# Two transformer blocks on one core: attention portions moved among k-steps, window scores of two heads in one portion, gate weights in one operand

## The reference

```python
# first block, per layer
h = rms_norm(x, g_pre);  proj = h @ w_in            # 2048 -> 6 k columns, split into heads
o_a = dense attention, 8 heads of 128, 2 key heads, norm and rope on q and k, * silu(a_g)
o_b = dense attention, 4 heads of 128+64, q and kv from low-rank latents,      * silu(b_g)
o_c = neighbourhood attention, 4 heads of 128, bias per position,             * silu(c_g)
x = x + rms_norm(concat(o_a, o_b, o_c) @ w_out, g_post)
# second block, per layer
h = rms_norm(x, g_pre) * (1 + scale) + shift;  proj = h @ w_in
y_a = sliding-window attention: 16 query heads of 64, 4 key heads, window 128, sinks
y_b = gelu(s_u) * spatial gating of gelu(s_v), chunks of 128
gate_logits = c_g @ gla_w_gate_up + gla_b_gate      # c_g: 16 columns of proj
log_alpha   = log_sigmoid(gate_logits) / 16
y_c = rms_norm(gated_linear_attention(c_q, c_k, c_v, log_alpha))
x = x + gate * rms_norm((concat(y_a, y_b, y_c) * silu(z)) @ w_out, g_post)
```

## Time and profile before

| | us |
| --- | --- |
| median of 3 runs | 3762.35 |
| lowest and highest | 3760.0, 3763.01 |
| the profiled execution's own time | 3766.83 |
| its span in the trace | 3765.1 |
| PE busy in it | 3553.3 (94%) |
| DVE, ACT, POOL busy | 1718.8, 1141.5, 1139.8 |
| mean granted clock of PE | 0.975 |

### The profile page before, as it was taken

The page is one execution under the profiler, slowest core; times in us unless marked ns, Lnnn a source line. Parts: engine busy times, 40 slices in busy tenths (PEclk is TensorE's granted clock), DMA queues, the critical chain, the costliest instruction groups (busy, mean ns, idle before and its releaser), DMA issues.

```text
span 3765.1 us, 52278 instructions
## 1 busy us (share of the span) xinstructions
PE 3553.3 (94%) x17005; PEld 2819.4 (75%) x17005; DVE 1718.8 (46%) x2884; ACT 1141.5 (30%) x1918; POOL 1139.8 (30%) x1242
## 2 busy tenths in 40 slices
PE   6999999999799999999997999999997999999998
PEld 5767777778686677777786778877786878877786
DVE  4533476443444236654425335544535334545533
ACT  3122333322321333332323234322323224322221
POOL 5664776560175477765300000012000000002000
PEclk9999999999899999999998999999998999999999
DMA  7444444453354354434432311322433322321332
GB/s 248 127 118 128 141 138 118 120 180 112 131 175 118 88 160 141 137 112 148 158 99 101 95 57 57 95 59 65 159 101 109 96 61 57 95 65 52 122 135 100
DMA packets 184717, 430.87 MB, mean 114 GB/s; under 512 B 21238, under 2 KB 26257, under 8 KB 178328
## 3 DMA queue, kind: packets, MB, share of 16 engines
q1 hardware_dynamic: 146344, 292.60, 24.7%
q0 software_dynamic: 33472, 109.06, 10.3%
q10 hardware_dynamic: 4656, 26.07, 1.8%
HBM read 406.58 MB, written 24.75 MB: 115 GB/s over the span
## 4 chain that ended last, share of the span: by engine, by line
PE 89%; DVE 5%; issue 3%; ACT 1%; DMA 1%; DVEq 0%; ACTq 0%; SPq 0%; POOL 0%; POOLq 0%
PE bank L699 22%; PE bank L701 21%; PE bank L700 21%; PE bank L772 4%; PE bank L792 3%; PE bank L758 2%; PE bank L878 2%; PE bank L694 2%; PE bank L781 2%; PE bank L696 1%; PE bank L695 1%; PE bank L718 1%; PE bank L899 1%; PE bank L1031 1%; PE bank L950 1%
## 5 line engine op out<-in xcount | busy, mean ns | idle before, releaser
L699 PE MATMUL bank<-wlo,act_hi 128*128 128x512 f32 (+1 forms) x3712 | 1531.8, 413 | 1.5 <-DVE zone L1530 0.9
L701 PE MATMUL bank<-whi,act_lo 128*128 128x512 f32 (+1 forms) x3712 | 1448.0, 390 | 0.0
L700 PE MATMUL bank<-whi,act_hi 128*128 128x512 f32 (+1 forms) x3712 | 1446.6, 390 | 0.0
L1475 DVE TENSOR_TENSOR wlo<-stage,whi 128x1024 fp32r<-128x1024 f32 (+1 forms) x496 | 670.0, 1357 | 730.1 <-ACT whi L1116 718.2
L699 PEld LDWEIGHTS bank<-wlo,act_hi 128*128 128x128 f32 x3712 | 704.1, 190 | 205.8 <-issue 63.2
L700 PEld LDWEIGHTS bank<-whi,act_hi 128*128 128x128 f32 x3712 | 704.7, 190 | 153.4 <-issue 24.7
L701 PEld LDWEIGHTS bank<-whi,act_lo 128*128 128x128 f32 x3712 | 702.5, 189 | 149.1
L1116 ACT ACTIVATE whi<-stage 128x1024 fp32r<-128x1024 f32 (+1 forms) x496 | 514.0, 1044 | 779.7 <-PE bank L701 381.6
L2291 POOL TENSOR_TENSOR macc<-macc,mprod 128x512 f32<-128x512 f32 x360 | 497.5, 1382 | 66.5 <-POOL mprod L2284 66.5
L2284 POOL TENSOR_SCALAR mprod<-wmod,csil 128x512 f32<-128x512 f32 x384 | 310.2, 808 | 296.6 <-PE bank L815 192.8
L2328 POOL DMA_DIRECT2D macc<-in_gla_w_gate_up x2 | 1.1, 542 | 1189.2 <-DVE Y L1948 1189.2
(11 more groups left out here) (255 smaller groups left out, 3244.0 us busy)
## 6 DMA issues: line engine op xcount, KB each, us to landing
stage<-in_w_in SPq DMA_DIRECT2D x352, 512.0 KB, 3.7
wmod<-in_w_mod POOLq DMA_DIRECT2D x384, 256.0 KB, 3.1
stage<-in_w_out SPq DMA_DIRECT2D x128, 512.0 KB, 3.8
out<-Y ACTq DMA_DIRECT2D x20, 1024.0 KB, 5.0
zone<-out SPq DMA_DIRECT2D x4, 4096.0 KB, 14.9
stage<-in_w_in SPq DMA_DIRECT2D x16, 320.0 KB, 3.7
Y<-in_x SPq DMA_DIRECT2D x4, 1024.0 KB, 10.2
rpb_tiles<-rpb_pad POOLq DMA_DIRECT2D x16, 224.0 KB, 4.9
```

The lines of the kernel that those rows point to most:

```text
L699: pe.matmul(out, hi_x, lo_w, start=(k == 0), stop=False)
L700: pe.matmul(out, hi_x, hi_w, start=False, stop=False)
L701: mm = pe.matmul(out, lo_x, hi_w, start=False, stop=(k == KC - 1))
L1475: dve.tensor_tensor(wlo[:, j % RH, :, 0:width], stage[:, j % RS, :, 0:width], whi[:, j % RH, :, 0:width].bitcast(F32), ALU.subtract).then_ ...
```

## The change

Lines of the changed kernel from L671 on are 7 to 10 higher than before.

- First block: the steps of units and jobs move. No scores are issued on steps whose `pv` would fall on k = 4 or 5, so none on k = 0 and 1; `UNIT_PV` goes from 3 to 4. The jobs of branch B come 1 to 3 steps later, AK goes from s = 112 to 117, AQ to a new list, the norms and ropes 1 to 3 steps later.
- Second block, window scores: the scores of the duos d and d + 1 are issued in one portion, on the step of the even d, the two heads by turns. Duos 0 and 1 of a quad are now the two heads of the first token pair. The wait is for the exponential of d (d - 1 counted from the duo ahead), the queries' wait for that of 4g.
- c_g: `cgw_hi` and `cgw_lo` become the two halves of one operand of 32 columns, `JOB_CG` has 32 matmuls, the gate matmul contracts over 32 rows with `gate_w` loaded twice.
- Levels: the steps skip k = 15 and k = 0, and what hangs on them moves along.

```diff
+UNIT_TURN, UNIT_PV, ROW_SUM = 2, 4, 4
+def unit_steps(first, n):
+    free = [s for s in range(first, first + 2 * n) if (s + UNIT_PV) % KC not in (ROW_SUM, ROW_SUM + 1)]
+    return free[:n]
+AQ_JOBS = (124, 131, 136, 141, 148, 153, 158, 165)
-for first, steps in ((U_B, [48, *range(51, 64), 64, 67]), (U_C, [*range(83, 97), 99, 100]),
-                     (U_A, [123, 124, 125, 126, 128, 131, 132, 133, 135, 136, 137, 138, 140, 141, 142, 143,
-                            147, 148, 149, 150, 152, 153, 154, 155, 157, 158, 159, 160, 163, 164, 165, 166])):
+for first, steps in ((U_B, unit_steps(50, 16)), (U_C, unit_steps(83, 16))):
     UNIT_AT.update({s: first + i for i, s in enumerate(steps)})
-UNIT_TURN, UNIT_PV = 2, 3
+for h in range(A_H):
+    UNIT_AT.update({s: U_A + 4 * h + i for i, s in enumerate(unit_steps(AQ_JOBS[h] + 1, 4))})
-for first, steps in ((J_CQ, (20, 21, 22, 23)), (J_QPE, (24, 25, 26, 27)), (J_QN, (28, 29, 30, 31)),
-                     (J_QPT, (33, 33, 34, 34)), (J_CKV, (35, 36, 37)), (J_KN, (38, 39, 40, 41)),
-                     (J_VB, (42, 43, 44, 45)), (J_AK, (112, 113)), (J_AQ, (122, 127, 134, 139, 144, 151, 156, 161))):
+for first, steps in ((J_CQ, (23, 24, 25, 26)), (J_QPE, (27, 28, 29, 30)), (J_QN, (31, 32, 33, 34)),
+                     (J_QPT, (36, 36, 37, 37)), (J_CKV, (38, 39, 40)), (J_KN, (41, 42, 42, 43)),
+                     (J_VB, (43, 44, 44, 45)), (J_AK, (117, 118)), (J_AQ, AQ_JOBS)):
-CQ_AT, QROPE_AT, CKV_AT = 17, 28, 32
+CQ_AT, QROPE_AT, CKV_AT = 17, 31, 35
-A_LOAD_AT, AK_AT, AQ_AT = 105, 106, (114, 130)
+A_LOAD_AT, AK_AT, AQ_AT = 105, 107, (116, 131)
...
-LEVEL_AT = 74
-OUT_AT = {91: 0, 93: 1, 106: 2, 108: 3}
-SQ_AT, SCALE_AT = 110, 113
+LEVEL = [s for s in range(74, 120) if s % KC not in (KC - 1, 0)][:4 * (LEVELS + 1) + 1]
+OUT_AT = {LEVEL[17]: 0, LEVEL[19]: 1, LEVEL[28] + 3: 2, LEVEL[28] + 5: 3}
+SQ_AT, SCALE_AT = LEVEL[28] + 7, LEVEL[28] + 10
...
-        score_done = count("score_done", UNITS, DUOS)
+        score_done = count("score_done", UNITS, DUOS // 2)
...
-            return 8 * (g // 4) + g % 4 + 4 * (d % 4 // 2)
+            return 8 * (g // 4) + g % 4 + 4 * (d % 2)
...
         JOB_CG = [(w, x) for k in range(KC) for w, x in
-                  ((cgw_hi[:, k, :], act_lo[:, k, :]), (cgw_hi[:, k, :], act_hi[:, k, :]),
-                   (cgw_lo[:, k, :], act_hi[:, k, :]))]
+                  ((cgw_r[:, k, :], act_hi[:, k, :]), (cgw_r[:, k, 0:G_RANK], act_lo[:, k, :]))]
...
-                    pe.wait_ge(exp_done.sem, exp_done.at(1, l, 4 * g - 1))
+                    pe.wait_ge(exp_done.sem, exp_done.at(1, l, 4 * g))
...
                 if d >= 2:
-                    pe.wait_ge(exp_done.sem, exp_done.at(1, l, d - 1))
-                for n, ks, cols_ in units_of(d):
-                    mm = pe.matmul(bank[4 + d % 2][:, cols_], qT_s[half, g % 2, tok(n)],
-                                   kT_s[half, g // 4, ks[0] * P:(ks[-1] + 1) * P], start=True, stop=True)
+                    pe.wait_ge(exp_done.sem, exp_done.at(1, l, d))
+                for i in range(2):
+                    for e in range(2):
+                        n, ks, cols_ = units_of(d + e)[i]
+                        half = slice(e * S_D, (e + 1) * S_D)
+                        mm = pe.matmul(bank[4 + e][:, cols_], qT_s[half, g % 2, tok(n)],
+                                       kT_s[half, g // 4, ks[0] * P:(ks[-1] + 1) * P], start=True, stop=True)
                 mm.then_inc(score_done.sem, 1)
...
-                if s in DUO_AT:
+                if s in DUO_AT and DUO_AT[s] % 2 == 0:
                     swa_scores(l, DUO_AT[s])
...
-                dve.wait_ge(score_done.sem, score_done.at(1, l, d + 1))
+                dve.wait_ge(score_done.sem, score_done.at(1, l, d // 2 + 1))
...
-                pool.dma_start(gate_w[0:G_RANK, :], io["gla_w_gate_up_2"][one].rearrange("o r n -> (o r) n"))\
-                    .then_inc(gate_in.sem, 16)
+                for i in range(2):
+                    pool.dma_start(gate_w[i * G_RANK:(i + 1) * G_RANK, :], io["gla_w_gate_up_2"][one].rearrange("o r n -> (o r) n"))\
+                        .then_inc(gate_in.sem, 16)
```

More of the change, by code:

```diff
@@ L106, in slot_of @@
     return k + k // LEVELS
-DECAY_AT = {(CUM_AT + 5 + k if k < 2 else LEVEL_AT - 4 + 2 * slot_of(k)): k for k in range(2 * LEVELS)}
-SCALED_AT = {(LEVEL_AT - 10 if k == 0 else LEVEL_AT - 2 + 2 * slot_of(k)): k for k in range(2 * LEVELS)}
+DECAY_AT = {(CUM_AT + 5 + k if k < 2 else LEVEL[2 * slot_of(k) - 4]): k for k in range(2 * LEVELS)}
+SCALED_AT = {(64 if k == 0 else LEVEL[2 * slot_of(k) - 2]): k for k in range(2 * LEVELS)}
 GELU_A, GELU_B = 0.044715, 0.7978845608028654
@@ L253, in build @@
         cgw = sb("cgw", [P, KC, G_RANK], at=wmod_at + 2432)
-        cgw_hi = sb("cgw_hi", [P, KC, G_RANK], F32R, at=sb_at["mprod"])
-        cgw_lo = sb("cgw_lo", [P, KC, G_RANK], F32R, at=sb_at["mprod"] + 4 * KC * G_RANK)
+        cgw_r = sb("cgw_r", [P, KC, 2 * G_RANK], F32R, at=sb_at["mprod"])
+        cgw_hi, cgw_lo = cgw_r[:, :, 0:G_RANK], cgw_r[:, :, G_RANK:2 * G_RANK]
         junk = sb("junk", [P, PW], at=sb_at["macc"])
@@ L343, in build @@
         sink_in = count("sink_in", 0, 16)
-        gate_in = count("gate_in", 0, 16 * 2)
+        gate_in = count("gate_in", 0, 16 * 3)
         sg_in = count("sg_in", 0, 16 * 4)
@@ L500, in units_of @@
             units, at = [], 0
-            for n in (2 * (d % 2), 2 * (d % 2) + 1):
+            for n in (2 * (d % 4 // 2), 2 * (d % 4 // 2) + 1):
                 ks = [n] if n == 0 else [n - 1, n]
@@ L870, in swa_scores @@
             def swa_scores(l, d):
-                g, half = d // 4, slice(d % 4 // 2 * S_D, (d % 4 // 2 + 1) * S_D)
+                g = d // 4
                 if d % 4 == 0:
@@ L906, in gate_logits @@
                 if pr == 0:
-                    pe.wait_ge(gate_in.sem, gate_in.at(1, l, 32))
+                    pe.wait_ge(gate_in.sem, gate_in.at(1, l, 48))
                     pe.wait_ge(pt_done.sem, pt_done.at(1, l, DUOS))
@@ L910, in gate_logits @@
                 for i in range(2):
-                    mm = pe.matmul(bank[6 + pr][:, i * 256:(i + 1) * 256], cgT[0:G_RANK, tok(2 * pr + i)],
-                                   gate_w[0:G_RANK, :], start=True, stop=True)
+                    mm = pe.matmul(bank[6 + pr][:, i * 256:(i + 1) * 256], cgT[0:2 * G_RANK, tok(2 * pr + i)],
+                                   gate_w[0:2 * G_RANK, :], start=True, stop=True)
                 mm.then_inc(job_done.sem, 1)
@@ L1081, in side @@
                     chunk_out(l, OUT_AT[s])
-                g = s - LEVEL_AT
+                g = LEVEL.index(s) if s in LEVEL else -1
                 if 0 <= g < 4 * (LEVELS + 1):
@@ L1097, in _ @@
                 for r, (lhs, rhs) in enumerate(JOB_CG):
-                    mm = pe.matmul(bank[4][0:G_RANK, :], lhs, rhs, start=(r == 0), stop=(r == len(JOB_CG) - 1))
+                    mm = pe.matmul(bank[4][0:lhs.shape[-1], :], lhs, rhs, start=(r == 0), stop=(r == len(JOB_CG) - 1))
                 mm.then_inc(job_done.sem, 1)
@@ L1913, in take_logits_in @@
                 dve.wait_ge(job_done.sem, job_done.at(1, l, J_CG + 1))
-                dve.tensor_copy(cgT[0:G_RANK, :], bank[4][0:G_RANK, :]).then_inc(job_ev.sem, 1)
+                dve.tensor_copy(cgT[0:2 * G_RANK, :], bank[4][0:2 * G_RANK, :]).then_inc(job_ev.sem, 1)
             def swa_take_keys(l, c):
@@ L1940, in swa_finish @@
             def swa_finish(l, d):
-                h, r, n0 = head_of(d), d % 4, 2 * (d % 2)
+                h, r, n0 = head_of(d), d % 4, 2 * (d % 4 // 2)
                 dve.wait_ge(pv_done.sem, pv_done.at(1, l, d + 1))
```

1 line of the change is left out of this document (removed).

## The result

The changed kernel takes 3720.45 us (median of 4 runs, 3705.07 to 3725.17), the kernel before 3761.18 (4 runs, 3759.04 to 3763.01). The ratio is 0.9885, with a 95% interval of 0.9855 to 0.9914. So 41 us are saved, not 77: the time lies outside the range of 3660 to 3714. The four runs are scattered over 20 us, where the four of before lie within 4; in the groups of the experiments, nine runs of the kernel before lie 5 to 14 apart.

What follows compares the result with a forecast made beforehand. PE, busy 94% of the span, was taken to bound the kernel. Savings of 34.4 + 7.4 + 27.3 - 1.0 + 9.1 - 0.6 = 76.6 us from the median 3762.35 gave 3685.8, range 3660 to 3714.

Steps and rivals of the forecast that it cites:

- Window scores in pairs: Second block: a pair of duos costs like one duo, a quad 20.9 in place of 23.08 us; 34.4 us saved.
- c_g: Gate matmuls ahead of panel 3: sixteen fewer per layer at 0.23 us each; 7.4 us saved.
- the second load: Gate weights loaded twice: the spatial gating's transfers come one later, 0.5 us per layer; 1.0 us lost.
- Level steps: Second block, ends of panels 7 and 8: waits and lower clock go, 13.6 us per layer; 27.3 us saved.
- The mask chain: DVE's gates and mask against the next level portion at k = 1: a draw, nothing or a few tenths.
- First block, jobs: Turns of QPT and AK wait less for DVE's ropes: 6.1 of 11.1 and 3.0 of 14.9 us; 9.1 us saved.
- First block, units: Waits of `pv`: 4.7 us per layer saved, 4.8 lost at panel 8's end, 0.2 at panel 9's; 0.6 us lost.
- The first block changed by over 15 us: Sign against the prediction: it would be wrong with the first block changed by over 15 us either way.
- more such stops: First block, ends of panels 3 and 5: `pv` waits behind the outcopy, 2 to 3 us each; 3697 us, chance 0.06.
- serial halves: Second block's paired window scores: row halves don't overlap, pairs gain 11 in place of 34.4 us; 3709 us, chance 0.10.
- level ends: Level ends keep a wait, mask chain late at k = 1, lower clock stays: half of 27.3; 3699 us, chance 0.08.
- pairs that wait: Second block: a pair's scores wait for both exponentials of the pair ahead; 3782 us with 3 us at each, chance 0.02.

Runs made afterwards that it cites:

- the two runs of the parts alone: The kernel before with only the paired window scores, 3730.68 us; the kernel before with only the level steps kept off k = 15 and 0, 3733.5 us.

## Why the prediction was right in one half and wrong in the other

- **Window scores in pairs**, 34.4 forecast: 30.5. The quad came out at 21.0 for 20.9. Most of the rest is in waits of this part for ACT that were shorter before: 1.3, 1.2 and 0.7 us (L898, L874, L888), of which 0.6 was there before. A pair costs what one duo cost, as the level steps had said; the loss that the Trainium skill's 3.07 of 4 for row tiles would mean (TensorE: Matmul & The Clock Gate, Part 3, Measured speedup) doesn't show.
- **c_g** 7.4 and **the second load** -1.0: 8.7 left over for both; 7.4 for c_g in the trace.
- **Level steps**, 27.3 forecast: 27.7. The mask chain, which I had called a draw, holds up nothing.
- **First block, jobs**, 9.1 saved forecast. The step said that PE waits for DVE and that more steps give DVE more time. For the turns that held: their 26.0 fell to 16.4, where about 17 was forecast. But 14.8 came up at L706, for which the sum had nothing: 9.8 of it at s = 115, where the key rope as one lump delays `split_lo`, 2.3 at s = 123 and 2.6 at s = 21. So these stops come to 31.2, and the 9.1 weren't there. I had seen the lump and had put all of its price at the turns of s = 124. The later experiments bear the mechanism out: with the rope cut up and the turns another step or two later no stop in panel 7 is over 1.7.
- **First block, units**, 0.6 lost forecast. This is the step that failed, and with it the term of 0.6. It named the right place and the right cause for panel 8, `finish` behind the gates at s = 143, with a wait of 5.5; it was 6.29 (4.86 in layer 1), and then the `pv`, the scores and the next step's first main matmuls ran at the lower clock. What it took for even was panel 9, "-0.2 on average": there the stop moved from s = 160 to 159 and grew from 3.65 to 6.56, and the panel cost 10.4 and 9.6 us. What it took for saved, the stop of 2.1 at s = 135, came back at s = 137 with 2.3 and the lower clock; that stop was never part of the 18.3 of the earlier trace rows from which the step took it, but of the 4.1 beside it. And the clock, priced at about 1 per layer, took 13.8 in the whole of the first block. Branch A's new tables, jobs and units together, cost 28.9 where I had them near nothing; the loss lies in panels 8 and 9. The first block changed by over 15 us, which the prediction had named as a sign that it is wrong.
- **What the sum left out altogether** is that DVE's own times aren't fixed. I took 5.65 for the gates from one execution. They were 7.05 after the change, and 4.9 where GpSimd stood still. A stop that is set by DVE work beside GpSimd's carries that with it; before the change most of the waits of `pv` were for ACT, and the one at s = 143 is 1.8 with the old tables whether GpSimd adds or not.

The rival "more such stops" (0.06, 3697) was the nearest in kind, though not in its number; it had them at panels 3 and 5, not at 8 and 9. The rivals of the second block (serial halves, level ends, pairs that wait) are all refuted by the quad and the two runs of the parts alone.

Open is whether the 20 us of scatter is anything of the new tables. They alone on the kernel before vary by 8 in five runs, not by the 10 or more that I expected, and the kernel before varies by 11 in the nine runs beside them. The kernel with the additions away varies by 9 with the new tables and by 4 with the old ones; five runs each don't show that the phase between GpSimd and DVE makes the difference.

## What to carry to other kernels

When a table moves portions, follow every dependence of a moved portion to the engine that serves it in order, and see what now stands ahead of it there; one lump (a panel's gates, a rope over all tiles) ahead of a tiny `finish` costs PE the whole lump and, here, half its clock for 5.7 us afterwards. Keep portions off the steps around such lumps, and give the lump's consumer more steps than its time says, or cut it up. Price DVE's work beside a busy GpSimd by several of its executions, not by one. Price by the neighbouring part that already has the new form (the level steps for the pairs, panel 9's end for the others): those terms held within 4 us.
